# Spreading the attention heads' reciprocal sums over partitions by two DMAs instead of TensorE transposes

## The chip, the cores and the metric

The kernel runs on one core of one Trainium2 chip. The metric is the device time in microseconds from the start of one execution to its end; the median of several executions is compared.

## The reference, cut to what matters

The program is one layer of a decoder trunk: forgetting attention with 16 heads of width 64 over 1,024 tokens of width 1,024, a layer norm, a mixture of 64 experts, and a second layer norm. The change touches the attention alone, and in it the division of a head's weighted values by its sums of exponentials:

```python
logits = einsum('bqhd,bkhd->bhqk', q[:, t0:t1], k[:, :t1]) * scale
logits = logits + c[:, :, t0:t1, None] - c[:, :, None, :t1]
p = softmax(where(causal, logits, -inf), axis=-1)          # per head and query
outs.append(einsum('bhqk,bkhd->bqhd', p, v[:, :t1]))
...
return o @ w_out
```

## The kernel before, in words

All engines are programmed by hand with semaphores; each engine runs its own list of instructions in order and waits where the list says so. Every matrix product is split in a high and a low part, so that one product is three matmuls (`split_matmul`, L91 to L93).

**A head.** `head(p, par)` is one of 16 heads, h = 2p + par. Heads 0 and 1 and the last two are written out, heads 2 to 13 are a loop over pairs. A head has eight steps t, one for each tile of 128 queries. In a step TensorE (PE) makes the scores of that tile (L864 to L867, one or two slots of up to 512 keys; 12 slots in a head), then transposes blocks of exponentials of earlier slots ("turns", L894) and projects a part of the next head's queries and keys (L91 to L93). VectorE (DVE) takes the maxima of the scores (L1681), ScalarE (ACT) the exponentials with their sums (L1290). ACT copies a turned slot out of PSUM as `pt_hi` (L1301), and DVE subtracts for `pt_lo` (L1692).

**The order of the turns** is a table, `TURNS`, and `STEP_TURNS` says which of its entries come in which step. Slots 8 and 9 of the head before are turned in step 0 of the next head, slots 10 and 11 in step 1, slot 0 in step 2, and so on up to slots 6 and 7 in step 7. Turns alternate between the two banks of the PSUM tile `k_ps`; a turn waits until `pt_lo` of the turn before it in its bank is made (`bank_free`).

**The weighted values.** `weigh_v(h, par, half)` (L916) multiplies the values with the turned exponentials of four query tiles into `pv_ps`, half of the PSUM tile `out_ps`. The first half is made in step 7 of head h and the second in step 3 of head h + 1. The result is transposed: 64 partitions hold the head's columns from the values' high part, 64 those of the low part, and the queries lie along the free axis. ACT copies the low part to `heads_sum` (`low_values`, L1309), and DVE adds the high part (`sum_halves`, L1707), which counts `added`. `weigh_v` waits for `added` of the half before, since both use `pv_ps`.

**The reciprocals.** The sums of the exponentials lie the other way, one query per partition: `ssum[par]` is 128 x 2 x 8. `reciprocals` (L1698, L1702) makes `rec[par]`, 128 x 8, half 0 in step 6 of its head and half 1 in step 1 of the next. To multiply `heads_sum` by them, 64 partitions must each hold a row of 512 reciprocals. Before the change PE makes it: the two entries `("rows", -1, 0)` in step 2 and `("rows", -1, 1)` in step 5 of the next head are four transposes each of a column of `rec` read 64 times (L901), into a bank of `k_ps`. `by_rows` (L1714) multiplies `heads_sum` with that bank into `attn`, which is the profile's tile `xs`, and counts `normed`. DVE does `normalise`, that is `sum_halves` and then `by_rows`, for half 0 in step 2 after the turn's `pt_lo` and for half 1 in step 5 before it.

**After the last head** PE turns the last slots, weighs the last half, and goes on with the output projection (`first_tile_out`, `out_projection`). GpSimd (POOL) sits in a wait for `normed` through all of the attention; then it makes constants and fills tables in memory.

**DMAs.** All of the attention's transfers are issued from SP's queue: the next head's weights `wqk`, values `va`, and per half the copies `q_ones` and `k_twice` between partitions.

Of the kernel before, what the change touches and what calls it, by code (L numbers as in the profile page):

```python
# [47 lines left out]
def turned_blocks(n):  # L48
# [47 lines left out]
def build(nc, x, w_in, b_f, w_out, ln1_g, ln1_b, router, router_bias, w_gate, w_up, w_down, ws_gate, ws_up,  # L96
          ws_down, ln2_g, ln2_b, out):
    with ExitStack() as ctx:
# [16 lines left out]
        v_dram = nc.dram_tensor("v_scratch", (T, HEADS, 2 * DH), F32, kind="Internal").ap()  # L115
        c_dram = nc.dram_tensor("c_scratch", (2, HEADS, T), F32, kind="Internal").ap()
# [10 lines left out]
        ones_b = sb("ones_b", [P, P], BF16)  # L127
        before = sb("before", [P, P], BF16)
# [3 lines left out]
        with ExitStack() as early:  # L132
# [3 lines left out]
            with ExitStack() as x1s:  # L136
# [21 lines left out]
                with ExitStack() as b:  # L158
# [5 lines left out]
                    heads_sum = sb("heads_sum", [DH, BANK], c=b)  # L164
# [3 lines left out]
                    rsum = sb("rsum", [P, TT // 2], c=b)  # L168
                    rec = [sb(f"rec{i}", [P, TT], c=b) for i in range(2)]
            with ExitStack() as d:  # L170
# [60 lines left out]
                zeros = sb("zeros", [P, ROW_W], c=d)  # L231
                nblk = [sb(f"nblk{i}", [1, E], c=d) for i in range(2)]
# [53 lines left out]
        for n in ("masks xt_ps xt_hi_ok xt_lo_ok wf_in wf_ok gate_ps g1_in gate_step zexp_ok"  # L286
                  " c_hi_ok c_lo_ok c_stored wv_hi_ok wv_lo_ok v_ps v_hi_ok v_ok"
                  " wqk_hi_ok wqk_lo_ok proj c_in ev_hi ev_lo copied score max_step maxed exped turned_ps turned_hi turned_lo rows_ps rec_step rec_ok"
# [43 lines left out]
        def load_v(sp, h, par):  # L332
            sp.dma_start(va[par][:].bitcast(F32), v_rows[:, :, bass.ds(h, 1), :].rearrange("p t o n -> p t (o n)")).then_inc(va_in[par], 16)

# [37 lines left out]
        def stand(eng):  # L372


            eng.sem_inc(S["stands"], 1)
# [209 lines left out]
        def _(pool):  # L585
# [24 lines left out]


            pool.wait_ge(S["normed"], NORMED)
# [170 lines left out]
        def _(pe):  # L783
# [86 lines left out]
            def bank_free(h, u, there):  # L870

                past = [v for v in range(u - 2, -1, -2) if there(TURNS[v])]
                if past:
                    kind, back, n = TURNS[past[0]]
                    if kind == "turn":
                        pe.wait_ge(S["turned_lo"], NS * h + (NS * back + n + 1))
                    else:
                        pe.wait_ge(S["normed"], 2 * h + (2 * back + n + 1))
# [4 lines left out]
            def turns(h, par, us, first=False, ends=False):  # L883
                for u in us:
                    kind, back, n = TURNS[u]
# [1268 lines left out]
```

## Time and profile before

| | us |
|---|---|
| median of 3 executions | 1645.97 |
| lowest and highest | 1644.61, 1650.76 |
| span of the profiled execution, first to last instruction | 1640.5 |
| attention heads, first scores to last `by_rows` | about 136 to 562 |

The profile gives the span alone of the execution that it shows; a measured time has some microseconds before and after the span too. On the profile's timeline a matmul's duration overlaps the next one's, so that its cost is read from start to start: a 512-column matmul is shown with 0.39 us and the next starts 0.23 us later. A bracket at the end of a line gives the idle time ahead of an instruction and what released it; an instruction can have waited without a bracket, because the modelled end of the one before it covers the wait. `x4` is four instructions merged in one line.

### The profile page before, as it was taken

How to read it: one execution, taken by the hardware profiler on the slowest of the kernel's cores; microseconds unless marked ns; L12 is line 12 of the kernel's file. 1: busy time of each engine (PE TensorE's matmuls, PEld its weight loads, DVE VectorE, ACT ScalarE, POOL GpSimd, SP SyncE). 2: the span in 40 equal slices, each digit the busy share in tenths (PEclk: the TensorE clock that was granted, in tenths of full speed). 3: DMA queues.
4: the chain of work that ended last, by engine and by line, in shares of the span. 5: the costliest groups of instructions: out<-in, count | busy, mean ns of one | idle time of the engine just before them, and what ended most of it. 6: DMA issues, size and time to landing. Idle time of an engine off the chain costs nothing.

```text
span 1640.5 us, 32188 instructions
## 1 busy us (share of the span) xinstructions
PE 1578.0 (96%) x8246; PEld 1310.0 (80%) x8247; DVE 1182.3 (72%) x2036; ACT 1032.5 (63%) x1706; POOL 503.7 (31%) x495
## 2 busy tenths in 40 slices
PE   6999999999999999899999999999999999999986
PEld 6897888888887788778878888888888888888863
DVE  4214777777777788847777787777876787888866
ACT  3214666666666655527677787666776777877854
POOL 0000000000000135432544454543454445454426
PEclk9999999999999999899999999999999999999995
DMA  7223222222123533657999999999999999999987
GB/s 245 91 81 91 72 48 68 58 65 71 45 71 103 170 134 138 227 196 281 337 291 318 305 357 367 326 289 264 334 318 288 274 353 331 342 368 370 367 252 282
DMA packets 161320, 368.63 MB, mean 225 GB/s; under 512 B 53009, under 2 KB 73489, under 8 KB 161265
## 3 DMA queue, kind: packets, MB, share of 16 engines
q1 hardware_dynamic: 136272, 284.21, 49.7%
q0 software_dynamic: 24992, 83.73, 19.7%
q8 instruction: 28, 0.46, 0.1%
q14 instruction: 28, 0.22, 0.0%
HBM read 294.39 MB, written 65.11 MB: 219 GB/s over the span
## 4 chain that ended last, share of the span: by engine, by line
PE 72%; DVE 8%; DMA 8%; issue 5%; ACT 3%; ACTq 2%; POOL 1%; SPq 0%; DVEq 0%; POOLq 0%
PE bank_pair L1025 6%; PE bank_pair L1031 6%; PE bank_pair L1028 6%; DMA sums_scratch<-ys,sidx 5%; PE q_ps L91 4%; PE q_ps L93 4%; PE q_ps L92 4%; PE out_ps L916 4%; PE k_ps L894 4%; PE out_ps L1084 3%; PE out_ps L1085 3%; PE q_ps L1015 3%; PE k_ps L1052 2%; PE k_ps L1053 2%; PE k_ps L1060 2%
## 5 line engine op out<-in xcount | busy, mean ns | idle before, releaser
L1918 DVE TENSOR_TENSOR gu_lo<-raw_gu,gu_hi 128x1024 fp32r<-128x1024 f32 x260 | 306.3, 1220 | 25.5 <-ACT gu_hi L1396 25.5
L1396 ACT CAST gu_hi<-raw_gu 128x1024 fp32r<-128x1024 f32 x260 | 253.2, 1050 | 2.3 <-DMA raw_gu<-in_moe_w_gate_dram 1.5
L1025 PE MATMUL bank_pair<-gu_hi,xb_hi 128*128 128x512 f32 x576 | 233.1, 405 | 5.5 <-DVE gu_lo L1918 4.2
L1028 PE MATMUL bank_pair<-gu_lo,xb_hi 128*128 128x512 f32 x576 | 226.9, 394 | 0.0
L682 POOL DMA_INDIRECT sums_scratch<-ys,sidx x63 | 122.1, 1939 | 148.9 <-DMA sums_scratch<-ys,sidx 116.0
L1918 DVE TENSOR_TENSOR dn_lo<-raw_dn,dn_hi 128x1024 fp32r<-128x1024 f32 x130 | 152.6, 1213 | 2.9 <-ACT dn_hi L1396 2.4
L1031 PE MATMUL bank_pair<-gu_hi,xb_lo 128*128 128x512 f32 x576 | 142.7, 390 | 2.0 <-DVE xb_lo L1922 2.0
L1301 ACT CAST pt_hi<-k_ps 128x512 fp32r<-128x512 f32 (+1 forms) x192 | 85.7, 482 | 75.4 <-PE k_ps L894 74.7
L1025 PEld LDWEIGHTS bank_pair<-gu_hi,xb_hi 128*128 128x128 f32 x576 | 110.1, 191 | 28.8 <-issue 6.4
L613 POOL IOTA e<- 128x64 f32 x1 | 0.2, 185 | 428.8 <-DVE xs L1714 428.8
L1396 ACT CAST dn_hi<-raw_dn 128x1024 fp32r<-128x1024 f32 x130 | 130.0, 1052 | 2.9 <-DMA raw_dn<-in_moe_w_down_dram 2.9
L1031 PEld LDWEIGHTS bank_pair<-gu_hi,xb_lo 128*128 128x128 f32 x576 | 108.0, 188 | 24.8 <-DVE xb_lo L1922 2.4
L1028 PEld LDWEIGHTS bank_pair<-gu_lo,xb_hi 128*128 128x128 f32 x576 | 109.7, 190 | 21.1
L657 POOL DMA_INDIRECT x_rows<-rows_scratch,gidx x64 | 77.4, 1210 | 154.2 <-DVE wcol L1934 122.6
L1692 DVE TENSOR_TENSOR pt_lo<-k_ps,pt_hi 128x512 fp32r<-128x512 f32 (+1 forms) x192 | 100.4, 551 | 27.8 <-ACT pt_hi L1301 27.0
L1052 PE MATMUL k_ps<-dn_hi,ht_hi 128*128 128x512 f32 x288 | 118.4, 411 | 0.0
L1053 PE MATMUL k_ps<-dn_lo,ht_hi 128*128 128x512 f32 x288 | 112.5, 391 | 0.0
L91 PE MATMUL q_ps<-xt_hi,wqk_hi 128*128 128x512 f32 x256 | 109.2, 427 | 0.0
L1290 ACT ACTIVATE probs<-bank_pair,nm 128x512 f32<-128x512 f32 (+3 forms) x128 | 74.7, 586 | 43.2 <-DVE nm L1685 29.7
L1084 PE MATMUL out_ps<-gu_hi,xo 128*128 128x512 f32 x248 | 97.3, 392 | 4.5 <-DVE xo L1938 4.5
L93 PE MATMUL q_ps<-xt_hi,wqk_lo 128*128 128x512 f32 x256 | 100.5, 393 | 0.0
L92 PE MATMUL q_ps<-xt_lo,wqk_hi 128*128 128x512 f32 x256 | 100.3, 392 | 0.0
(306 smaller groups left out, 3973.7 us busy)
## 6 DMA issues: line engine op xcount, KB each, us to landing
raw_gu<-in_moe_w_gate_dram SPq DMA_DIRECT2D x128, 512.0 KB, 6.8
raw_gu<-in_moe_w_up_dram SPq DMA_DIRECT2D x128, 512.0 KB, 8.6
raw_dn<-in_moe_w_down_dram SPq DMA_DIRECT2D x128, 512.0 KB, 8.3
wqk<-in_fox_w_in_dram SPq DMA_DIRECT2D x66, 128.0 KB, 2.5
v_scratch<-v_out SPq DMA_DIRECT2D x32, 256.0 KB, 2.8
va<-v_scratch SPq DMA_DIRECT2D x16, 512.0 KB, 4.7
fin<-sums_scratch SPq DMA_DIRECT2D x16, 512.0 KB, 8.3
xs<-in_x_dram SPq DMA_DIRECT2D x8, 512.0 KB, 7.4
```

The lines of the kernel that those rows point to most:

```text
L91: pe.matmul(out, w_hi, m_hi, start=start, stop=False, skip_group_check=True)
L92: pe.matmul(out, w_hi, m_lo, start=False, stop=False, skip_group_check=True)
L93: return pe.matmul(out, w_lo, m_hi, start=False, stop=stop, skip_group_check=True)
L682: g.indirect_dma_start(out=sums[0], out_offset=bass.IndirectOffsetOnAxis(ap=sidx[par][:, 0:1], axis=0), in_=ys[par][:], in_offset=None, co ...
L1025: i = pe.matmul(o3, xb_hi[s][:, c], g_hi[:, :, c], start=c == 0, stop=False, skip_group_check=True)
L1028: pe.matmul(o3, xb_hi[s][:, c], g_lo[:, :, c], start=False, stop=False, skip_group_check=True)
L1031: i = pe.matmul(o3, xb_lo[s][:, c], g_hi[:, :, c], start=False, stop=c == DC - 1, skip_group_check=True)
L1052: pe.matmul(k_ps[:, r], ht_hi[:, c], d_hi[:, c, r], start=c == 0, stop=False, skip_group_check=True)
L1053: pe.matmul(k_ps[:, r], ht_hi[:, c], d_lo[:, c, r], start=False, stop=False, skip_group_check=True)
L1084: pe.matmul(o3, xo[:, c], g_hi[:, :, c], start=c == 0, stop=False, skip_group_check=True)
L1396: a.copy(hi, raw).then_inc(S[done], 1)
L1918: dve.tensor_tensor(lo, raw, hi, ALU.subtract).then_inc(S[lo_ok], 1)
```

## The change

PE's eight transposes per head are gone, and with them the `rows` entries of `TURNS`; the other turns stay in their steps. POOL, for each head and half, waits for `rec_ok`, stores the 128 x 4 reciprocals to a row of 512 numbers in memory (`rec_scratch`), so that query 128t + p stands at that place, waits for the store, and loads the row into 64 partitions of a new tile `rec_rows`, partitions 0 to 63 for half 0 and 64 to 127 for half 1. Before the store it waits until the load before it has landed and until the multiplication that last used this half of `rec_rows` is done. `by_rows` waits for the load (`rows_in`) and reads `rec_rows` from SBUF instead of the bank. `heads_sum` has 128 partitions now, a half for each half, and ACT's wait in `low_values` is looser by one. Two constants of POOL, `ones_b` and `before`, are made after the attention.

```diff
-TURNS = [("turn", -1, 8), ("turn", -1, 9), ("turn", -1, 10), ("turn", -1, 11), ("turn", 0, 0), ("rows", -1, 0), ("turn", 0, 1),
-         ("turn", 0, 2), ("rows", -1, 1)] + [("turn", 0, n) for n in range(3, 8)]
-STEP_TURNS = [(0, 1), (2, 3), (4, 5), (6,), (7,), (8, 9), (10, 11), (12, 13)]
+TURNS = [("turn", -1, 8), ("turn", -1, 9), ("turn", -1, 10), ("turn", -1, 11), ("turn", 0, 0), ("turn", 0, 1),
+         ("turn", 0, 2)] + [("turn", 0, n) for n in range(3, 8)]
+STEP_TURNS = [(0, 1), (2, 3), (4,), (5,), (6,), (7,), (8, 9), (10, 11)]
...
+        rec_dram = nc.dram_tensor("rec_scratch", (2, BANK), F32, kind="Internal").ap()
...
-                    heads_sum = sb("heads_sum", [DH, BANK], c=b)
+                    heads_sum = sb("heads_sum", [P, BANK], c=b)
+                    rec_rows = sb("rec_rows", [P, BANK], c=b)
...
+            def spread_reciprocals(p, par, first=False):
+
+                h = 2 * p + par
+                for half in range(2):
+                    n = 2 * h + half
+                    pool.wait_ge(S["rec_ok"], n + 1)
+                    if not (first and half == 0):
+                        pool.wait_ge(S["rows_in"], 32 * n)
+                    if not first:
+                        pool.wait_ge(S["normed"], n - 1)
+                    stand(pool)
+                    pool.dma_start(rec_dram[half].rearrange("(t p) -> p t", p=P), rec[par][:, half * 4:half * 4 + 4],
+                                   allow_slow_non_contiguous=True).then_inc(S["rows_in"], 16)
+                    pool.wait_ge(S["rows_in"], 32 * n + 16)
+                    stand(pool)
+                    pool.dma_start(half_rows(rec_rows, half), rec_dram[half:half + 1, :].to_broadcast([DH, BANK])).then_inc(S["rows_in"], 16)
+            spread_reciprocals(0, 0, first=True)
+            spread_reciprocals(0, 1)
+            with pool.Fori(1, PAIRS) as p:
+                for par in range(2):
+                    spread_reciprocals(p, par)
+
+            pool.wait_ge(S["normed"], NORMED)
             g.memset(ones_b[:], 1.0).then_inc(S["c_const"], 1)
...
-                    else:
-                        pe.wait_ge(S["rec_ok"], 2 * h + (2 * back + n + 1))
-                        stand(pe)
-                        for j in range(4):
-                            t = 4 * n + j
-                            i = pe.transpose(bank[0:DH, j * P:(j + 1) * P], rec[of][:, t:t + 1].to_broadcast([P, DH]), ident[:])
-                        i.then_inc(S["rows_ps"], 1)
...
-            turns(HEADS, 0, (2, 3, 5), ends=True)
+            turns(HEADS, 0, (2, 3), ends=True)
             weigh_v(HEADS - 1, 1, 1)
-            turns(HEADS, 0, (8,), ends=True)
             first_tile_out(DC - 1)
...
-                if not (static(h) and 2 * h + half == 0):
-                    act.wait_ge(S["normed"], 2 * h + half)
-                a.copy(heads_sum[:], pv_ps[DH:P, :]).then_inc(S["low_ok"], 1)
+                if not (static(h) and h == 0):
+                    act.wait_ge(S["normed"], 2 * h + (half - 1))
+                a.copy(half_rows(heads_sum, half), pv_ps[DH:P, :]).then_inc(S["low_ok"], 1)
...
-                dve.wait_ge(S["rows_ps"], 2 * h + (half + 1))
-                bank = key_banks[TURNS.index(("rows", -1, half)) % 2]
-                dve.tensor_tensor(attn[par * DH:(par + 1) * DH, bass.ds(p, 1), half * BANK:(half + 1) * BANK], heads_sum[:, None, :],
-                                  bank[0:DH, None, :], ALU.mult).then_inc(S["normed"], 1)
+                dve.wait_ge(S["rows_in"], 64 * h + (32 * half + 32))
+                dve.tensor_tensor(attn[par * DH:(par + 1) * DH, bass.ds(p, 1), half * BANK:(half + 1) * BANK], half_rows(heads_sum, half)[:, None, :],
+                                  half_rows(rec_rows, half)[:, None, :], ALU.mult).then_inc(S["normed"], 1)
```

## Rows read from the trace of the kernel before

**Rows 1.** The page of the profiled execution: its span, and the busy time of each engine.

```profile
span 1640.5 us, 32188 instructions
...
PE 1578.0 (96%) x8246; PEld 1310.0 (80%) x8247; DVE 1182.3 (72%) x2036; ACT 1032.5 (63%) x1706; POOL 503.7 (31%) x495
```

**Rows 2.** Busy time by stretch: PE, PEld, DVE, ACT, POOL, granted clock, DMA share, GB/s.

```profile
180.00:520.00 340.00, 338.26 (x1959) 282.54 (x1958) 258.40 (x545) 221.68 (x583) 0.00 (x0) 1.00 0.25 60
```

**Rows 3.** Timeline of PE, heads 6 and 7: start, us, engine, line, op.

```profile
305.97 0.60 PE L901 MATMUL k_ps<-ident,rec 128*64 128x128 f32 x4
306.40 0.60 PE L894 MATMUL k_ps<-ident,probs 128*128 128x128 f32 x4
...
314.85 0.23 PE L867 MATMUL bank_pair<-mask_qk,identb 128*128 128x128 bf16 x1
315.27 0.98 PE L894 MATMUL k_ps<-ident,probs 128*128 128x128 f32 x7 [0.19 <-DVE pt_lo L1692]
...
318.45 1.04 PE L894 MATMUL k_ps<-ident,probs 128*128 128x128 f32 x8
...
321.93 0.60 PE L901 MATMUL k_ps<-ident,rec 128*64 128x128 f32 x4
322.28 0.48 PE L91 MATMUL q_ps<-xt_hi,wqk_hi 128*128 128x512 f32 x1
...
324.64 0.47 PE L916 MATMUL out_ps<-pt_hi,va 128*128 128x512 f32 x1
```

**Rows 4.** Timeline of DVE in the same stretch.

```profile
305.71 1.02 DVE L1681 TENSOR_REDUCE nm<-bank_pair 128x1 f32<-128x512 f32 x2 [0.55 <-PE bank_pair L865]
...
307.82 0.68 DVE L1714 TENSOR_TENSOR xs<-heads_sum,k_ps 64x512 f32 x1 [0.27 <-DVE heads_sum L1707]
...
312.39 0.69 DVE L1627 TENSOR_TENSOR wqk_lo<-wqk,wqk_hi 128x512 fp32r<-128x512 f32 x1 [1.12 <-ACT wqk_hi L1251]
313.00 0.17 DVE L1698 RECIPROCAL rec<-ssum 128x4 f32<-128x4 f32 x1
...
314.46 1.01 DVE L1692 TENSOR_TENSOR pt_lo<-k_ps,pt_hi 128x512 fp32r<-128x512 f32 x2
...
321.11 0.18 DVE L1702 RECIPROCAL rec<-rsum 128x4 f32<-128x4 f32 x1
321.73 0.69 DVE L1672 SCALAR_TENSOR_TENSOR q_both<-q_ps,q_both 64x512 fp32r<-64x512 f32 x1 [0.44 <-ACT k_twice L1282]
...
323.82 0.67 DVE L1707 TENSOR_TENSOR heads_sum<-out_ps,heads_sum 64x512 f32<-64x512 f32 x1
324.64 0.68 DVE L1714 TENSOR_TENSOR xs<-heads_sum,k_ps 64x512 f32 x1
```

**Rows 5.** Timeline of ACT in the same stretch.

```profile
311.75 0.61 ACT L1251 CAST wqk_hi<-wqk 128x512 fp32r<-128x512 f32 x1
```

**Rows 6.** Timeline of PE where the last head begins.

```profile
520.57 0.23 PE L867 MATMUL bank_pair<-mask_qk,identb 128*128 128x128 bf16 x1
520.63 0.94 PE L894 MATMUL k_ps<-ident,probs 128*128 128x128 f32 x7
```

**Rows 7.** Timeline of all engines after the last head.

```profile
556.34 0.60 PE L901 MATMUL k_ps<-ident,rec 128*64 128x128 f32 x4 [1.65 <-DVE pt_lo L1692]
...
557.04 0.68 DVE L1714 TENSOR_TENSOR xs<-heads_sum,k_ps 64x512 f32<-64x512 f32 x1 [0.85 <-PE k_ps L901]
```

**Rows 8.** DVE groups by line and form, 180 to 520 us: count, busy us, mean ns.

```profile
L1627 DVE TENSOR_TENSOR wqk_lo<-wqk,wqk_hi 128x512 fp32r<-128x512 f32 x26 | 18.0, 692 | 15.0 <-ACT wqk_hi L1251 13.9
```

**Rows 9.** DMA issues of the whole run: count, KB each, median us to landing.

```profile
sums_scratch<-ys POOLq DMA_DIRECT2D x8, 512.0 KB, 4.1
```

**Rows 10.** DMA issues from 180 to 520 us.

```profile
q_ones<-q_both SPq DMA_DIRECT2D x26, 128.0 KB, 3.1
```

**Rows 11.** The tile tab_scratch: ns min/median/max of the issues, us to landing.

```profile
L635 POOL DMA_INDIRECT tab_scratch<-tok,dest_i x64: 965/969/1967, 595.8 to 719.3; - x64
...
DMA to landing us min/median/max: 2.1/2.4/7.1
```

More of the change, by code:

```diff
@@ L231, in build @@
                 zeros = sb("zeros", [P, ROW_W], c=d)
+                ones_b = sb("ones_b", [P, P], BF16, c=d)
+                before = sb("before", [P, P], BF16, c=d)
                 nblk = [sb(f"nblk{i}", [1, E], c=d) for i in range(2)]
@@ L287, in build @@
                   " c_hi_ok c_lo_ok c_stored wv_hi_ok wv_lo_ok v_ps v_hi_ok v_ok"
[L288 removed]
+                  " wqk_hi_ok wqk_lo_ok proj c_in ev_hi ev_lo copied score max_step maxed exped turned_ps turned_hi turned_lo rows_in rec_step rec_ok"
                   " pv low_ok added normed"
@@ L333, in load_v, with half_rows @@
             sp.dma_start(va[par][:].bitcast(F32), v_rows[:, :, bass.ds(h, 1), :].rearrange("p t o n -> p t (o n)")).then_inc(va_in[par], 16)
+        def half_rows(tile, half):
+            return tile[half * DH:(half + 1) * DH, :]
         def copy_halves(sp, h, par, half):
@@ L873, in bank_free @@
                 if past:
-                    kind, back, n = TURNS[past[0]]
-                    if kind == "turn":
-                        pe.wait_ge(S["turned_lo"], NS * h + (NS * back + n + 1))
-                    else:
-                        pe.wait_ge(S["normed"], 2 * h + (2 * back + n + 1))
+                    _, back, n = TURNS[past[0]]
+                    pe.wait_ge(S["turned_lo"], NS * h + (NS * back + n + 1))
                 elif not (static(h) and h == 0):
@@ L884, in turns @@
                 for u in us:
-                    kind, back, n = TURNS[u]
+                    _, back, n = TURNS[u]
                     if first and back:
                         continue
-                    of = par if back == 0 else 1 - par
                     bank = key_banks[u % 2]
                     bank_free(h, u, lambda x: not (first and x[1]) and not (ends and not x[1]))
-                    if kind == "turn":
-                        pe.wait_ge(S["exped"], NS * h + (NS * back + n + 1))
-                        for j in range(SLOTS[n][2] // P):
-                            i = pe.transpose(bank[:, j * P:(j + 1) * P], probs[n % PROBS][:, j * P:(j + 1) * P], ident[:])
-                        i.then_inc(S["turned_ps"], 1)
-                    else:
-                        pe.wait_ge(S["rec_ok"], 2 * h + (2 * back + n + 1))
-                        stand(pe)
-                        for j in range(4):
-                            t = 4 * n + j
-                            i = pe.transpose(bank[0:DH, j * P:(j + 1) * P], rec[of][:, t:t + 1].to_broadcast([P, DH]), ident[:])
-                        i.then_inc(S["rows_ps"], 1)
+                    pe.wait_ge(S["exped"], NS * h + (NS * back + n + 1))
+                    for j in range(SLOTS[n][2] // P):
+                        i = pe.transpose(bank[:, j * P:(j + 1) * P], probs[n % PROBS][:, j * P:(j + 1) * P], ident[:])
+                    i.then_inc(S["turned_ps"], 1)
             def weigh_v(h, par, half):
@@ L1327, in head @@
                     for u in STEP_TURNS[t]:
-                        if TURNS[u][0] == "turn" and not (first and TURNS[u][1]):
+                        if not (first and TURNS[u][1]):
                             turned_high(h, u)
@@ L1739, in head @@
                     for u in STEP_TURNS[t]:
-                        if TURNS[u][0] == "turn" and not (first and TURNS[u][1]):
+                        if not (first and TURNS[u][1]):
                             turned_low(h, u)
```

10 lines of the change are left out of this document (3 added, 7 removed).

## The prediction

> **What bounds the kernel now.** I read the page first. TensorE is busy for 96% of a span of 1640.5 us [rows 1], so any work taken from it looks like time. The windows come next, because a share over the whole span says nothing of one stage: through the heads PE is busy for 338.26 of 340.00 us at a granted clock of 1.00, DVE for 258.40, ACT for 221.68, and POOL does nothing [rows 2]. That again says PE. But a matmul's end is modelled and can hide a wait, so the third view is the timeline, read from start to start on PE, then on DVE and ACT for the same microseconds. The reader should look there at two places in each head at which PE waits for DVE though it is shown busy.
>
> *Place 1, step 0.* The last score matmul of head 7's step 0 starts at 314.85 and the turn of slot 8 at 315.27 [rows 3]. Where nothing is waited for these two lie 0.06 us apart [rows 6]. So PE stood still for 0.36 us, for `pt_lo` of slot 6, the first of the two that start at 314.46 [rows 4]. That wait has a history. DVE begins the maxima of step 5 at 305.71, having waited 0.55 us for PE's scores; goes through `heads_sum`, `by_rows` at 307.82 and the maxima of step 6; ACT makes the exponentials of step 6 from those and then `wqk_hi` at 311.75 [rows 5]; DVE waits 1.12 us for it, makes `wqk_lo` at 312.39, the maxima of step 7, and `pt_lo` at 314.46 [rows 4]. From 305.71 to 315.27 that chain takes 9.56 us; PE's own work beside it, from 305.97 to 314.91, takes 8.94.
>
> *Place 2, step 3.* `weigh_v` of the second half starts at 324.64 [rows 3], 0.15 us after `heads_sum` of half 0 ended on DVE at 323.82 + 0.67 = 324.49 [rows 4]: it may not overwrite `pv_ps` before. This chain begins with PE's turn of slots 10 and 11 at 318.45 [rows 3], goes through ACT's copies, exponentials and `k_twice`, for which DVE waited 0.44 us at 321.73, and through `k_rest`, the maxima of step 2 and `pt_lo` of slot 0 to `heads_sum` [rows 4].
>
> The timeline repeats this: the step-0 wait stands in heads 1 to 14 (0.2 to 0.4 us), the step-3 wait in all of heads 1 to 15. Only the start of head 15 has no wait: 520.57 to 520.63 [rows 6]. A head takes (520.63 - 315.27) / 8 = 25.67 us [rows 3, 6].
>
> **The change part by part.**
>
> *Transposes removed.* The four of half 1 in step 5 cost 306.40 - 305.97 = 0.43 us, the four of half 0 in step 2 cost 322.28 - 321.93 = 0.35 us [rows 3]. With 16 of each that is 16 x 0.78 = 12.5 us of PE time. Where they lie decides what it is worth.
>
> - Step 5, heads 1 to 13. They stand at 305.97, behind the scores that start DVE's chain at 305.71, and ahead of place 1. They shorten the 8.94 us and not the 9.56. PE comes 0.43 us earlier and waits 0.79 instead of 0.36. Worth 0.
> - Step 2, heads 1 to 15. They stand at 321.93, after the turn that starts the second chain and ahead of place 2. `heads_sum` does not need them, so `weigh_v` starts when it did. Worth 0; at the most the 0.1 us by which PE's wait there can be smaller than it looks.
> - Step 5 of head 14. Nothing is waited for at 520.63 [rows 6], since head 14 splits no further weights in step 6. Worth 0.43 us, which the following turns hand on.
> - Step 5 of head 15. There the output weights are split and PE waits for DVE's `wo_lo`. Worth 0.
> - After head 15. Four transposes at 556.34 stand straight ahead of `weigh_v`, and DVE's `by_rows` waited 0.85 us for them [rows 7]. Four more follow `weigh_v`. PE gains 2 x 0.35 = 0.7 at most. But the first tile's layer norm follows the last `by_rows`, which moves only by the 0.35 of `weigh_v`, and PE needs that tile next. I take 0.5, between the bounds 0.35 and 0.7.
>
> *by_rows.* It now reads both operands from SBUF. The nearest row of that form is `wqk_lo<-wqk,wqk_hi`, 692 ns [rows 8], against 680 ns for `by_rows` [rows 4]. In step 5 it lies in the chain of place 1: 13 x 0.012 = 0.2 us slower at most.
>
> By the Trainium skill (VectorE: DVE Perf Modes, The TRN2 errata — SBUF-src ops pay a fixed extra latency per instruction) VectorE pays 58 cycles fixed from SBUF and 120 from PSUM at 0.96 GHz, so `by_rows` would get 65 ns shorter and the kernel, as an estimate from that page, 13 x 0.065 = 0.8 us faster instead of 0.2 slower. The two rows of this case differ by 12 ns the other way, and they decide the sum.
>
> *Store and load.* No row shows such a pair. The store is 512 pieces of 4 bytes. The nearest row is POOL's scatter of 128 pieces of 4 bytes: landing 2.4 us after the issue starts, 2.1 at least and 7.1 at most, its issue 0.97 [rows 11]. If only the issue grows with the pieces, it is 4 x 0.97 - 0.97 = 2.9 us longer. I take 2.4 + 1.7 = 4.1. The load is 128 KB in 64 rows. SP's transfers of that form land in 3.1 us [rows 10], POOL's of 512 KB in 4.1 [rows 9]. I take 3.5. With two semaphore hops a pair takes X = 7.8 us. Lower bound 2.1 + 3.1 = 5.2; upper bound 7.1 + 4.1 = 11.2, or with the longer issue on top 14.1.
>
> What covers it: half 0's `rec` is ready at 313.17 and its `by_rows` starts at 324.64, 11.5 us later. Half 1's is ready at 321.29 and used in the next head at 307.82 + 25.67 = 333.5, 12.2 us later [rows 3, 4, 6]. But POOL does them one after the other: both pairs, from 313.17, must be through by 333.5, so 2X must be under 20.3 us and X under 10.2. With 7.8 nothing is late: cost 0, and 4.7 us to spare. Queued behind POOL's waits are only its constants, which nobody needs until after the attention. SP's queue keeps its order.
>
> *Other waits.* ACT's looser wait in `low_values` and the freer bank of `k_ps` bind nowhere in the loop. The two constants made later, on POOL, run while `dest_i` is far off. Worth 0.
>
> *Sum.* Against the profiled execution: 1640.5 - 0.43 - 0.5 + 0.1 = 1639.7. The median of the runs, 1645.97, lies 5.5 us above that span; the same distance gives 1645.1.
>
> **The rivals.**
>
> *A: PE really is the bound.* If the waits at places 1 and 2 shrink with PE's work, because DVE and ACT run on as PE feeds them earlier, all 12.5 us come: 1645.97 - 12.5 = 1633.5. For it: 96% and 338.26 of 340.00. If only the step-2 part came, 15 x 0.35 = 5.3 us: 1640. Against it: the chain of place 1 begins before the transposes, and DVE's own maxima keep ACT from starting sooner.
>
> *B: the rows come late (the other side).* X over 10.2. Then `by_rows` of half 1 waits on DVE, in front of `pt_lo` of slot 3 and the maxima of step 6, straight in the chain of place 1. ACT waits for these maxima and PE for `pt_lo`. Each head loses 2X - 20.3. It decides from X = 10.5, where 14 x 0.6 = 8.2 us are lost. At X = 11.2 it is 2.1 a head, 14 x 2.1 = 29: 1675. For it: a landing of 7.1 us for 4-byte pieces [rows 11] and four times as many pieces here. Against it: that was the maximum and the median is 2.4, and DMA is a quarter busy in this stretch [rows 2].
>
> The Trainium skill (SBUF — State Buffer, SBUF: two separate sides) has a rule that points this way: POOL's DMAs are described by software that cannot write descriptors while DVE runs a two-port copy. In the heads DVE runs no copy or cast, and no row has a POOL DMA here, so it is open. A wait for one DVE instruction of 0.69 us [rows 4] at each of the two DMAs would make X 9.2, still under 10.2.
>
> *C: the small packets disturb SP's copies.* `q_ones` and `k_twice` of half 1 are issued about when half 1's store is. They land in 3.1 us [rows 10] and step 4 needs them about 6 us after the issue. Were they 3 us late and 0.6 more, a head would lose 0.6: 1654.
>
> **How the numbers follow.** A half per cent, 8.2 us, is about what a measurement of this kernel tells from no change. Forecast 0.72, within 1643.5 and 1646.5: both places of PE's wait are read off three engines, and the cover of the DMAs is some 30% longer than they need. A 0.12, of which 0.10 full. B 0.12, C 0.04. A's small form at 1640 is inside the half per cent, so faster is 0.10, same 0.74, slower 0.16. The range reaches down to 1633 to take in A, and up to 1654, B's and C's beginning; it leaves out the rest of B, about 0.1, and some of A.
>
> **What would show it.** Right: no L901; PE's busy time about 12 us lower through the heads and the period of a head still 25.6 to 25.8; gaps before the step-0 turn near 0.8 us and before `weigh_v` near 0.5; `by_rows` never released by a DMA; store to landing of load 7 to 9 us. Wrong: a period near 24.9 (A); DVE's `xs` waiting for a DMA, a longer period (B); PE's step-4 scores released by `k_twice` (C). What would make me wrong above all is the price of 512 four-byte pieces, which no row has, or a chain on DVE and ACT that moves up with PE after all.

## The result, and the profile after

The changed kernel takes 1800.57 us (median of 4, 1794.85 to 1802.99) against 1646.53 for the kernel before beside it: 1.0932 times as long, 95% interval 1.0906 to 1.0958. It is slower by 154 us where 1645.1 was forecast.

Page of the changed kernel: span and busy times, the granted clock in 40 slices, the chain that ended last, the two groups of part 5 in which the loss stands (busy us and mean ns, then the idle time ahead and its releaser), and the values' DMA of part 6.

```profile
span 1796.9 us, 32138 instructions
PE 1604.8 (89%) x8118; PEld 1322.5 (74%) x8119; DVE 1187.9 (66%) x2036; ACT 1032.2 (57%) x1706; POOL 558.0 (31%) x559
PEclk9999898988888988998999999999999999999995
PE 38%; DMA 29%; issue 8%; DVE 8%; ACT 4%; ACTq 1%; POOL 1%; POOLq 1%; DVEq 1%; another core or an unknown queue 1%
DMA rec_scratch<-rec 15%; DMA rec_rows<-rec_scratch 8%; PE bank_pair L1036 5%; PE bank_pair L1039 5%; PE bank_pair L1042 5%; DMA sums_scratch<-ys,sidx 4%; PE out_ps L1095 3%; PE out_ps L1096 3%; PE q_ps L1026 3%; PE k_ps L1063 2%; PE k_ps L1064 2%; PE k_ps L1071 2%; DVE gu_lo L1928 2%; PE out_ps L1113 2%; PE out_ps L1114 1%
L913 PE MATMUL k_ps<-ident,probs 128*128 128x128 f32 x576 | 93.2, 286 | 106.0 <-DVE pt_lo L1703 105.9
L1724 DVE TENSOR_TENSOR xs<-heads_sum,rec_rows 64x512 f32 (+1 forms) x32 | 22.0, 686 | 137.4 <-DMA rec_rows<-rec_scratch 136.4
va<-v_scratch SPq DMA_DIRECT2D x16, 512.0 KB, 11.8
```

The new store and load hold 23% of the chain that ended last. DVE waited 136.4 us for the rows, and PE then 105.9 us for the `pt_lo` behind them. The window of [rows 2] now reads:

```profile
180.00:520.00 340.00, 260.76 (x1354) 211.37 (x1353) 193.17 (x398) 161.96 (x425) 25.69 (x40) 0.87 0.27 54
```

PE is busy for 260.76 us in place of 338.26, and has done 1354 instructions in place of 1959. One head on POOL's timeline (start, us, then in brackets the idle time ahead and what ended it), and the lines of DVE and PE at its end:

```profile
399.99 0.79 POOL L621 DMA_DIRECT2D rec_scratch<-rec  x1 [10.99 <-DVE rec L1709]
408.62 0.53 POOL L625 DMA_DIRECT2D rec_rows<-rec_scratch  x1 [7.85 <-DMA rec_scratch<-rec]
413.01 0.79 POOL L621 DMA_DIRECT2D rec_scratch<-rec  x1 [3.85 <-DMA rec_rows<-rec_scratch]
423.02 0.53 POOL L625 DMA_DIRECT2D rec_rows<-rec_scratch  x1 [9.23 <-DMA rec_scratch<-rec]
434.87 0.79 POOL L621 DMA_DIRECT2D rec_scratch<-rec  x1 [11.32 <-DVE rec L1709]
```
```profile
399.07 0.17 DVE L1709 RECIPROCAL rec<-ssum 128x4 f32<-128x4 f32 x1
...
412.48 0.68 DVE L1724 TENSOR_TENSOR xs<-heads_sum,rec_rows 64x512 f32 x1 [1.15 <-DMA rec_rows<-rec_scratch]
...
428.76 0.69 DVE L1724 TENSOR_TENSOR xs<-heads_sum,rec_rows 64x512 f32 x1 [7.64 <-DMA rec_rows<-rec_scratch]
...
433.95 0.17 DVE L1709 RECIPROCAL rec<-ssum 128x4 f32<-128x4 f32 x1
```
```profile
430.23 0.47 PE L913 MATMUL k_ps<-ident,probs 128*128 128x128 f32 x1 [7.32 <-DVE pt_lo L1703]
```

The loss can be read off these lines. Half 0's reciprocals are ready at 399.07 + 0.17 = 399.24, and half 1's `by_rows` starts at 428.76. In between lie 0.75 us up to the first store's issue, then store (8.63), load (4.39), store (10.01) and load (5.74), one after the other: 29.5 us. The kernel before left 20.3 us for them. This head is a usual one: from store to load it is 8.1 to 11.2 us over all 32 stores, 9.8 at the median. From that `by_rows` to the next reciprocals' end takes 434.12 - 428.76 = 5.36 us, as before (313.17 - 307.82 = 5.35, [rows 4]). So a head takes 29.5 + 5.4 = 34.9 us in place of 25.7 [rows 3, 6], 9.2 more, and 16 x 9.2 = 147. The last `by_rows` ends at 712.2, against 562.0 before: 150 of the 154 us are in the heads.

The clock fell with the waits. Windows of the same kernel:

```profile
402.50:408.50 6.00, 6.00 (x37) 5.13 (x35) 3.94 (x9) 4.40 (x12) 0.00 (x0) 1.00 0.00 0
```
```profile
420.00:425.00 5.00, 2.91 (x17) 2.17 (x15) 1.05 (x3) 2.31 (x6) 0.53 (x1) 1.00 0.40 56
425.00:430.00 5.00, 0.00 (x0) 0.00 (x0) 1.21 (x2) 0.00 (x0) 0.00 (x0) 0.56 0.42 106
430.00:435.00 5.00, 4.77 (x13) 3.49 (x14) 3.67 (x9) 2.11 (x6) 0.13 (x1) 0.50 0.00 0
```

PE waited 7.32 us up to its matmul at 430.23, and within that wait the granted clock went from 1.00 to 0.50, that is from 2.4 to 1.2 GHz. It costs little here: DVE's part of the head took the same 5.36 us. The first of these lines shows something odder. From 402.5 to 408.5 the store has not yet released POOL, and yet the DMA engines' busy share is 0.00 and 0 GB/s move. From 399.9 to 408.6 the profile counts these packets for POOL's queue (packets, MB, share):

```profile
q0 software_dynamic: 32, 0.00, 0.7%
```

So all the packets that it shows of the store lie ahead of 402.5, and some 6 us pass after them in which it shows nothing. What takes the time is not carrying bytes.

### The profile page after: what moved, and what is told of

It is laid out like the page before. It is cut to its first block, busy times and chain, and to the rows that moved or that the text cites. A ratio compares the mean times of both kernels' runs of the same rounds, so it can differ in the third digit from the quotient of the medians.

```text
span 1796.9 us, 32138 instructions
## 1 busy us (share of the span) xinstructions
PE 1604.8 (89%) x8118; PEld 1322.5 (74%) x8119; DVE 1187.9 (66%) x2036; ACT 1032.2 (57%) x1706; POOL 558.0 (31%) x559
## 4 chain that ended last, share of the span: by engine, by line
PE 38%; DMA 29%; issue 8%; DVE 8%; ACT 4%; ACTq 1%; POOL 1%; POOLq 1%; DVEq 1%; another core or an unknown queue 1%
DMA rec_scratch<-rec 15%; DMA rec_rows<-rec_scratch 8%; PE bank_pair L1036 5%; PE bank_pair L1039 5%; PE bank_pair L1042 5%; DMA sums_scratch<-ys,sidx 4%; PE out_ps L1095 3%; PE out_ps L1096 3%; PE q_ps L1026 3%; PE k_ps L1063 2%; PE k_ps L1064 2%; PE k_ps L1071 2%; DVE gu_lo L1928 2%; PE out_ps L1113 2%; PE out_ps L1114 1%
## 5 line engine op out<-in xcount | busy, mean ns | idle before, releaser
L913 PE MATMUL k_ps<-ident,probs 128*128 128x128 f32 x576 | 93.2, 286 | 106.0 <-DVE pt_lo L1703 105.9
L913 PEld LDWEIGHTS k_ps<-ident,probs 128*128 128x128 f32 x576 | 66.1, 148 | 110.2 <-DVE pt_lo L1703 109.9
L681 POOL DMA_INDIRECT x_rows<-rows_scratch,gidx x64 | 81.8, 1278 | 146.3 <-DVE wcol L1944 115.4
L91 PE MATMUL q_ps<-xt_hi,wqk_hi 128*128 128x512 f32 x256 | 116.0, 453 | 0.0
L1724 DVE TENSOR_TENSOR xs<-heads_sum,rec_rows 64x512 f32 (+1 forms) x32 | 22.0, 686 | 137.4 <-DMA rec_rows<-rec_scratch 136.4
L93 PE MATMUL q_ps<-xt_hi,wqk_lo 128*128 128x512 f32 x256 | 107.1, 418 | 0.0
L92 PE MATMUL q_ps<-xt_lo,wqk_hi 128*128 128x512 f32 x256 | 106.9, 418 | 0.0
```

The lines of the kernel that those rows point to most:

```text
L91: pe.matmul(out, w_hi, m_hi, start=start, stop=False, skip_group_check=True)
L92: pe.matmul(out, w_hi, m_lo, start=False, stop=False, skip_group_check=True)
L93: return pe.matmul(out, w_lo, m_hi, start=False, stop=stop, skip_group_check=True)
L913: i = pe.transpose(bank[:, j * P:(j + 1) * P], probs[n % PROBS][:, j * P:(j + 1) * P], ident[:])
```

## The experiments

The loop issues 32 stores and 32 loads in all, one pair for each half of the 16 heads; where an expectation says 64 pairs or 64 stores, it is 32. "The heads end" is the end of the last `by_rows`, 562.0 us in the kernel before; it compares also where the output of the heads differs, and with it the experts' counts and the time behind the heads. It holds for one execution, and the first reciprocals of these executions lie between 154.5 and 158.6 us (158.3 in the kernel before), so that a difference of some 4 us says little. "A head" is the distance of half 0's reciprocals from heads 2 to 14, divided by 12.

**Is it the size of the pieces?** In this run each partition's four reciprocals go to memory as one piece of 16 bytes, and `by_rows` undoes the order by reading `rec_rows` with a step of four numbers.

```diff
-pool.dma_start(rec_dram[half].rearrange("(t p) -> p t", p=P), rec[par][:, half * 4:half * 4 + 4],
-               allow_slow_non_contiguous=True).then_inc(S["rows_in"], 16)
+pool.dma_start(rec_dram[half].rearrange("(p t) -> p t", p=P), rec[par][:, half * 4:half * 4 + 4]).then_inc(S["rows_in"], 16)
...
-dve.tensor_tensor(attn[par * DH:(par + 1) * DH, bass.ds(p, 1), half * BANK:(half + 1) * BANK], half_rows(heads_sum, half)[:, None, :],
-                  half_rows(rec_rows, half)[:, None, :], ALU.mult).then_inc(S["normed"], 1)
+dve.tensor_tensor(attn[par * DH:(par + 1) * DH, bass.ds(p, 1), half * BANK:(half + 1) * BANK].rearrange("q o (t p) -> q (o t) p", p=P),
+                  half_rows(heads_sum, half).rearrange("q (t p) -> q t p", p=P),
+                  half_rows(rec_rows, half).rearrange("q (p t) -> q t p", p=P), ALU.mult).then_inc(S["normed"], 1)
```

> The store writes each partition's four reciprocals as one piece of 16 bytes (128 pieces instead of 512 of 4 bytes), and by_rows reads rec_rows with a step of four, so that the result is the same. If the number of 4-byte pieces is the price: the store lands 2.5 to 3.5 us after its issue instead of 8 to 10, a pair takes about 7, nothing is late, and the time is 1645 +- 2, since by the prediction's steps the removed transposes are worth about 1 us. If PE's work was the bound after all: 1633. If any store and load on POOL's queue is slow whatever its pieces: about 1800 as with the change.

Measured: 1656.73 us, 1.0052 times the kernel before (1.0038 to 1.0066). Nearly all of the 154 us are gone. POOL's timeline of this run:

```profile
319.05 0.57 POOL L621 DMA_DIRECT2D rec_scratch<-rec  x1 [14.56 <-DVE rec L1708]
322.31 0.53 POOL L624 DMA_DIRECT2D rec_rows<-rec_scratch  x1 [2.69 <-DMA rec_scratch<-rec]
```

From store to load it is 3.26 us in place of 8.6 to 10. What is left has another cause: the heads end at 575.6, 13 us late, and DVE's groups of 180 to 520 us show it:

```profile
L1723 DVE TENSOR_TENSOR xs<-heads_sum,rec_rows 64x512 f32 (+1 forms) x26 | 27.9, 1072 | 7.0 <-DVE heads_sum L1717 5.9 <-DMA rec_scratch<-rec 1.1
```

Read with a step, `by_rows` takes 1072 ns in place of 686, and 32 x 0.386 = 12.4 us is about the delay.

**What are the removed transposes worth?** No DMA at all; `rec_rows` is filled once with a constant, so that the heads are not normalised.

```diff
-            spread_reciprocals(0, 0, first=True)
-            ...
+            pool.wait_ge(S["rec_ok"], 1)
+            g.memset(rec_rows[:], 0.01).then_inc(S["rows_in"], 1)
...
-                dve.wait_ge(S["rows_in"], 64 * h + (32 * half + 32))
+                dve.wait_ge(S["rows_in"], 1)
```

> The change without its two DMAs: rec_rows is filled once with a constant, so the values are not normalised by their sums. This is what the removed transposes are worth by themselves. By the prediction's steps (both places shadowed by the DVE and ACT chain): 1645 +- 2, a head still 25.6 to 25.8 us, the gap before the step-0 turn near 0.8 us. If PE's work sets the pace: 1633.5, a head 24.9.

Measured: 1662.38 us for the kernel, ratio 1.0086 (1.0069 to 1.0103). The 14 us lie behind the heads, whose output is another one here; the heads end at 562.8. Window:

```profile
180.00:520.00 340.00, 330.86 (x1842) 268.25 (x1841) 257.64 (x540) 220.77 (x581) 0.00 (x0) 1.00 0.25 60
```

PE is busy for 7.4 us less here than in [rows 2] and stands still for as much longer; the heads end no sooner, and from their first reciprocals they take 406.7 us against 403.7 before. Taken away alone, the transposes were worth nothing.

**What do the DMAs do when `by_rows` does not wait for them?** The kernel before, transposes included, with POOL's stores and loads as in the change, and `by_rows` reading PE's rows. One wait stays, in the last line: DVE's `reciprocals` may overwrite `rec` only when the load of two heads before has landed (in the runs without a load, the store). "Unwaited" below means this.

```diff
+            spread_reciprocals(0, 0, first=True)
+            spread_reciprocals(0, 1)
+            with pool.Fori(1, PAIRS) as p:
+                for par in range(2):
+                    spread_reciprocals(p, par)
...
+                if not (static(h) and h < 2):
+                    dve.wait_ge(S["rows_in"], 64 * h + (32 * half + 32 - 128))
```

> The kernel before, transposes and all, and beside them POOL's stores and loads of the change into a tile that nobody reads. Nobody waits for them, except that rec is not overwritten two heads later before its store has gone. If the loss of the change is that by_rows waits for the rows: 1646 to 1650. If it is that the small pieces hold up SP's copies (q_ones, k_twice, which landed up to 11.6 us after issue with the change and are needed some 6 us after it): up to 5 us a head more, 1690 to 1720, with PE's or DVE's waits put down to k_twice or q_ones.

Measured: 1728.83 us, ratio 1.0483 (1.0465 to 1.0500), 80 us slower. The heads end at 617.6, 56 us late; POOL itself, behind with its pairs, comes out of them only at 667.0, and the stage behind the heads needs it. The waits of this run from 200 to 520 us (total, times, longest):

```profile
POOL rec_rows L622 <- DMA rec_scratch<-rec: 192.9, 19, 11.2
...
PE bank_pair L886 <- DMA k_twice<-k_twice: 23.5, 8, 5.6
```

Not all of the 80 us is a disturbance of other transfers. The pairs take longer than a head, POOL falls behind, and the one wait that stayed binds in the last heads (136 to 720 us):

```profile
DVE ssum L1724 <- DMA rec_rows<-rec_scratch: 20.0, 4, 11.1
DVE rec L1722 <- DMA rec_rows<-rec_scratch: 1.6, 1, 1.6
```

That is 21.6 of the 56 us in the heads, and the other 24 of the 80 come behind them, where POOL is late. Some 34 us are left for what the transfers do to others.

**Is it the number of pieces?** The changed kernel with 128 pieces of 4 bytes per store instead of 512, loaded four times over, so that the rows of all but one tile of 128 queries are another tile's.

```diff
-pool.dma_start(rec_dram[half].rearrange("(t p) -> p t", p=P), rec[par][:, half * 4:half * 4 + 4],
+pool.dma_start(rec_dram[half, 0:P].rearrange("(p t) -> p t", p=P), rec[par][:, half * 4:half * 4 + 1],
```

> The change with a store of only one of the four columns of reciprocals, 128 pieces of 4 bytes, repeated four times by the load (256 pieces of 512 bytes): three quarters of the queries get another tile's reciprocal. If the price goes with the number of pieces: the store lands after about 3.5 us (2 us fixed and a quarter of the 7 us above it), nothing is late, 1645. If it goes with 4-byte writes as such: 8 us and about 1800.

Measured: 1844.09 us, ratio 1.1188 (1.1166 to 1.1209); the heads end at 726.4. A quarter of the pieces, and POOL's timeline shows a store that is hardly cheaper:

```profile
407.70 0.54 POOL L621 DMA_DIRECT2D rec_scratch<-rec  x1 [11.04 <-DVE rec L1709]
415.06 0.63 POOL L625 DMA_DIRECT2D rec_rows<-rec_scratch  x1 [6.82 <-DMA rec_scratch<-rec]
421.57 0.54 POOL L621 DMA_DIRECT2D rec_scratch<-rec  x1 [5.88 <-DMA rec_rows<-rec_scratch]
430.56 0.63 POOL L625 DMA_DIRECT2D rec_rows<-rec_scratch  x1 [8.44 <-DMA rec_scratch<-rec]
```

7.4 and 9.0 us from store to load, and 8.6 at the median of all 32 against 9.8. A price per piece falls with this run. That the heads end even later than with the change (712.2) goes with the load: it is written in four parts here and takes 6.5 us (415.06 to 421.57) in place of 4.4. What the dear stores have in common is that their 4-byte pieces lie packed, one beside the other, so that is what the next three runs vary, unwaited.

**Unwaited, 16 bytes.** The run of 1728.83 with the 16-byte store of the first one.

> The kernel before, with TensorE's turned reciprocals as they were, and the 64 pairs of store and load issued on Pool's queue with nobody waiting for their data: the same as the run that cost 1728.8 us with 4-byte pieces, but each store now writes 128 pieces of 16 bytes. Theory (what is dear is a run of 4-byte writes packed densely in memory, which holds up the other transfers of the queues): the stores land in under 3 us, the copies of q and k on SP's queue keep their 3.1 us, and the kernel is at 1646 to 1651. Rival (any store and load every 12.8 us disturbs SP's copies, 64-fold broadcast included): at least 1680. A small disturbance that the changed kernel's own waits had covered would stand between, near 1655.

Measured: 1642.40 us, ratio 0.9968 (0.9953 to 0.9984); store landing 2.5 us after its issue at the median. Nothing is disturbed by 32 pairs as such, the broadcast loads included. That the ratio lies under 1 is not explained: the heads end at 561.4 as before.

**Unwaited, 4 bytes, each in 64 bytes of its own, no load.**

```diff
-rec_dram = nc.dram_tensor("rec_scratch", (2, BANK), F32, kind="Internal").ap()
+rec_dram = nc.dram_tensor("rec_scratch", (2, BANK * 16), F32, kind="Internal").ap()
...
-pool.dma_start(rec_dram[half].rearrange("(t p) -> p t", p=P), rec[par][:, half * 4:half * 4 + 4],
+pool.dma_start(rec_dram[half].rearrange("(t p s) -> p t s", p=P, s=16)[:, :, 0], rec[par][:, half * 4:half * 4 + 4],
```

> The kernel before plus 64 unread stores on Pool's queue and no load: 512 pieces of 4 bytes as in the change, but each piece in 64 bytes of its own (the scratch tensor is 16 times as large). Theory A (pieces that share a stretch of memory are written one after another): the store lands in 3 to 4 us and the kernel is at 1646 to 1652. Theory B (4-byte writes are dear as such, wherever they lie): the store keeps its 8 to 10 us and the kernel is at 1700 to 1730. The run with 128 pieces, which kept 8.2 us, speaks against a price per piece, so A is thought likelier, at 60 to 40.

Measured: 1644.42 us, ratio 0.9974 (0.9954 to 0.9993). The tile's view:

```profile
L618 POOL DMA_DIRECT2D rec_scratch<-rec x32: 752/752/989, 159.5 to 551.2; - x32
...
DMA to landing us min/median/max: 2.2/3.1/3.6
```

The same 512 pieces, the same bytes, the same issue time, and a landing of 3.1 us.

**Unwaited, 4 bytes packed, no load.** As the last one, with the change's own store.

> The kernel before plus the same 64 unread stores of 512 dense 4-byte pieces, and no load. Theory (the store alone is what holds up SP's transfers): most of the 80 us of the run with both transfers stay, 1700 to 1730. Rival (the 64-fold broadcast load of 128 KB, 64 packets more per pair, is the disturbing part): under 1665.

Measured: 1677.41 us, ratio 1.0176 (1.0144 to 1.0208); the heads end at 591.6. Less than expected: the packed store alone costs 29 us. That is near the 34 that were left of the 80 for disturbed transfers; the load behind a cheap store cost nothing (1642.40). What the load adds behind a dear one was not taken apart further. The 29 us do not come evenly: six of the fifteen distances from head to head are 4.6 to 6.4 us longer than in the kernel before, the other nine as they were. The DMA issues from 200 to 650 us (count, KB each, median us to landing), and one of the places at which PE pays:

```profile
q_ones<-q_both SPq DMA_DIRECT2D x26, 128.0 KB, 4.9
k_twice<-k_twice SPq DMA_DIRECT2D x26, 128.0 KB, 5.5
```
```profile
416.60 0.50 PE L883 MATMUL bank_pair<-k_twice,q_both 128*128 128x512 f32 x1 [4.04 <-DMA k_twice<-k_twice]
```

All of PE's waits for `k_twice` in this run, from 200 to 520 us:

```profile
PE bank_pair L883 <- DMA k_twice<-k_twice: 13.5, 4, 4.0
```

SP's copies land in 3.2 us each in the same stretch of the kernel before. Here they take 4.9 and 5.5, though they are on another queue, and the slowest `k_twice` 13.2 in place of 4.7. The Trainium skill (DMA: Bandwidth & Descriptors, Back-pressure in remote DMA) says that stalled writes stall the other queues of the same DMA engine too. It says so of transfers between cores; this run's landings, 5.5 in place of 3.2, agree for local ones.

**The place in memory, in the changed kernel itself.** All of the change kept, its waits, load and DVE's multiplication; each 4-byte piece in 64 bytes of its own, by the same edit; ahead of the heads two DMAs fill the larger tensor once. The load reads the first 512 numbers of that larger tensor, so the heads are not normalised by their own sums.

> The changed kernel with its 512 pieces of 4 bytes per store, its waits, its load of 128 KB and its multiplication on DVE all kept; only each piece lies in 64 bytes of its own. The load reads the first 512 words of that tensor, which hold few of the reciprocals, so the heads are not normalised, and the counts of the experts behind them differ: the end of the heads is what compares (562.0 us in the kernel before, 711.5 plus 0.69 in the changed one). Theory (the whole loss is the dense 4-byte store): store and load together take 7 us, nobody waits, the heads end at 562 to 566. Rival (512 packets and a broadcast load with waits between them cost of themselves, in the changed order of the instructions): the heads end beyond 580.

Measured: 1646.87 us, ratio 1.0016 (0.9999 to 1.0034); the heads end at 565.1. POOL's timeline:

```profile
401.10 0.79 POOL L621 DMA_DIRECT2D rec_scratch<-rec  x1 [4.37 <-DVE rec L1716]
404.74 0.53 POOL L625 DMA_DIRECT2D rec_rows<-rec_scratch  x1 [2.85 <-DMA rec_scratch<-rec]
```

Of the 150 us in the heads 147 hang on where 512 small pieces lie. The load, too, is faster behind such a store: it lands in 2.8 us at the median. In this run the change behaves as forecast, in time too, though the counts of the experts behind the heads are not the same.

**The order of instructions, in the kernel before.** If the two places bind, moving their chains forward should help. The first two edits are ScalarE's, the last is DVE's.

```diff
-                        take(h, par, 1)
                         low_values(h - 1, 0)
+                        take(h, par, 1)
...
-                    elif t == 6 and left > 2:
+                    elif t == 5 and left > 2:
                         weights_hi(h + 2, 0)
...
                     if t == 2 and not first:
-                        normalise(h - 1, *before_it, 0)
+                        by_rows(h - 1, *before_it, 0)
                     if t == 1 and not first:
                         reciprocals(h - 1, 1 - par, 1)
+                        sum_halves(h - 1, 0)
```

> The kernel before with its transposes and three instructions of the chain DVE/ScalarE moved: the high weights of head h+2 from step 6 to step 5 of ScalarE, the low copy of head h-1 ahead of the score copy in step 1, and the sum of its two halves on DVE from step 2 to step 1. If the two places where TensorE waits in each head (step 0's turn for the low part, step 3's values for the sum) are what bounds the heads, about 0.2 to 0.4 us per head come off: 1635 to 1643. If TensorE's own work is the bound there, 1646 to 1650 as before.

Measured: 1650.39 us, ratio 1.0015 (1.0003 to 1.0028): no gain. PE's timeline shows why:

```profile
316.03 0.23 PE L867 MATMUL bank_pair<-mask_qk,identb 128*128 128x128 bf16 x1
316.10 0.94 PE L894 MATMUL k_ps<-ident,probs 128*128 128x128 f32 x7
...
325.01 0.23 PE L867 MATMUL bank_pair<-mask_qk,identb 128*128 128x128 bf16 x1
325.59 0.44 PE L894 MATMUL k_ps<-ident,probs 128*128 128x128 f32 x2 [0.35 <-DVE pt_lo L1692]
325.81 0.47 PE L916 MATMUL out_ps<-pt_hi,va 128*128 128x512 f32 x1
```

In step 0 the wait is gone: 0.07 us between the first two lines, where it was 0.42 [rows 3]. In step 3 `weigh_v` comes 0.22 us after its turn's start, where it was 0.37. But that turn itself now waits 0.5 us for a `pt_lo`, which is as much as was won at both places.

**A version that lets the transposes count.** The changed kernel with the 16-byte store, and `by_rows` on POOL, which is free there. POOL does it behind its load of the same half, and DVE's `reciprocals` wait until the multiplication two heads before is through (last line), since it no longer stands in DVE's own order.

```diff
+            def by_rows(h, p, par, half):
+                pool.wait_ge(S["added"], 2 * h + (half + 1))
+                pool.wait_ge(S["rows_in"], 64 * h + (32 * half + 32))
+                g.tensor_tensor(attn[par * DH:(par + 1) * DH, bass.ds(p, 1), half * BANK:(half + 1) * BANK].rearrange("q o (t p) -> q (o t) p", p=P),
+                                half_rows(heads_sum, half).rearrange("q (t p) -> q t p", p=P),
+                                half_rows(rec_rows, half).rearrange("q (p t) -> q t p", p=P), ALU.mult).then_inc(S["normed"], 1)
...
+                if not (static(h) and h < 2):
+                    dve.wait_ge(S["normed"], 2 * h + (half - 3))
```

> The changed kernel with two changes: the store writes 128 pieces of 16 bytes, and the multiplication by the rows (32 in all, one per half of a head) is done by Pool, which reads the rows with a step of four words, in place of DVE. TensorE's transposes stay removed. Theory (with cheap stores and no transposes the chain of DVE and ScalarE sets the pace of the heads, as the lengthened multiplication showed: 32 times 0.385 us by its step, and the heads ended 12.9 us later): taking 0.686 us twice a head off DVE lets TensorE's removed 12.5 us come through in part; the heads end at 552 to 558 us in place of 562.0 and the kernel is at 1636 to 1642. Rival 1 (the two places are held by other waits, the values' results for one): no gain, heads end at 562 to 565, 1645 to 1650. Rival 2 (Pool at work beside DVE slows DVE's own instructions): over 1652.

Measured: 1644.19 us, ratio 0.9988 (0.9975 to 1.0002). The heads end at 563.6, as in rival 1, 12 us before the same kernel with DVE's long `by_rows` and no sooner than the kernel before.

**Both together.** The same with the order of instructions moved as above (`by_rows` has left DVE, so `sum_halves` alone moves there).

> The kernel of the 16-byte store with Pool's multiplication, and the order of instructions moved as in the run of the reordered kernel before (that run: 1650.4 us, no gain): high weights of head h+2 in step 5 of ScalarE, the low copy of head h-1 ahead of the score copy in step 1, the sum of the halves on DVE in step 1. Theory: with TensorE's 12.5 us of transposes gone the waits at the two places are all that is left, so the moved instructions now help: 2 to 6 us below the same kernel without the reorder. Rival: they only move the wait to another step, as in the kernel before: within 2 us of it.

Measured: 1624.27 us, ratio 0.9863 (0.9842 to 0.9885). This beats both kernels, the one before by 22 us and the changed one by 176. The heads end at 547.6. Tile `rec` on DVE from 200 to 520 us, half 0's line, in the kernel before, in the run without the moved instructions and in the one with them:

```profile
L1698 DVE RECIPROCAL rec<-ssum x13: 167/171/174, 210.0 to 516.9; 128x4 f32<-128x4 f32 x13
```
```profile
L1718 DVE RECIPROCAL rec<-ssum x13: 167/171/172, 208.9 to 516.0; 128x4 f32<-128x4 f32 x13
```
```profile
L1718 DVE RECIPROCAL rec<-ssum x13: 164/170/172, 206.5 to 498.9; 128x4 f32<-128x4 f32 x13
```

A head takes (516.9 - 210.0) / 12 = 25.58 us in the kernel before, (516.0 - 208.9) / 12 = 25.59 with POOL's `by_rows` alone, and (498.9 - 206.5) / 12 = 24.37 with both edits: 1.21 less than before. PE's time for a head's transposes was 0.78, and its waits at the two places, as the prediction reads them, 0.36 and 0.15: 1.29 in all. So the transposes and the waits seem to come through together, and only here. PE is full again; its window of this run:

```profile
180.00:495.00 315.00, 313.68 (x1806) 263.51 (x1805) 241.40 (x503) 215.41 (x567) 67.95 (x78) 1.00 0.33 76
```

**Which of the two edits carries it?** The 16-byte store, DVE's own strided `by_rows`, and the moved instructions.

> The changed kernel with the 16-byte store and DVE's own multiplication (1.07 us, as in the run of the 16-byte store, 1656.7 us, heads ended about 575.7), and the three instructions moved as in the run with Pool's multiplication that came to 1624.3. It tells which of the two edits of that run carries its gain. If the moved instructions alone let TensorE's removed transposes come through: 1638 to 1644 (the 20 us of that run's reorder off 1656.7 would give 1637). If DVE must be relieved of the multiplication too: the strided 1.07 us twice a head keep DVE's chain the pace and the kernel stays at 1650 to 1657.

Measured: 1655.15 us, ratio 1.0043 (1.0028 to 1.0059); the heads end at 569.6. Neither does alone. By the heads' end, from 575.6 with the 16-byte store only: the order gives 6, POOL's `by_rows` 12, both together 28. By the head it is 26.42 us with the store only, 25.97 with the order, 25.59 with POOL's `by_rows`, 24.37 with both. That fits two places in a head, each of which holds it while the other is mended; which edit frees which place was not read off the traces.

## Why the prediction was wrong, point by point

*What bounds the heads: right.* The chains of DVE and ACT at the two places hold PE, not its own work. PE is shown busy for 99% of the window, and the run without DMAs bears out that its work does not set the pace. So does the long `by_rows`: 12.4 us more on DVE and the heads ended 13 us later. One size was off. Without DMAs PE's wait in step 0 of head 7 was to grow from 0.36 to 0.79 us and grew to 0.42 only, while the one ahead of `weigh_v` grew from 0.15 to 0.58.

*Transposes removed, worth 0.9 us: right to within 4.* The heads end at 562.8 against 562.0 without any DMA, and counted from their own beginning they take 3 us more. Rival A falls: it gave 12.5 us, and none came. Its gain comes once DVE and ACT are relieved at both places, which took both edits together (1624.27).

*by_rows 12 ns slower: close.* 686 ns against 680. It decides against the shorter access to SBUF that the prediction takes from the Trainium skill, as the two rows did there.

*Store and load, X = 7.8 us: this is the step that failed.* Measured: 29.5 us for two pairs, X = 14.8. The load was sized at 3.5 and took 4.4 and 5.7. The store was sized at 4.1 and took 8.6 and 10.0, over every bound that was worked out for it alone; only "with the longer issue on top", X = 14.1, came near. Two things were wrong in it. The scatter of [rows 11] was taken as the nearest row, because its pieces are of 4 bytes; but it is a different pattern, each of whose pieces goes to a place that an index gives, and no row of it shows what packed pieces cost. And the price was scaled by the number of pieces, in the issue. The issue grew to 0.79 us only, and with 128 pieces the store was nearly as dear as with 512. What counts is that 4-byte pieces are packed: in 64 bytes of their own the same 512 let the load go 3.64 us after the store's issue in the changed kernel. The load's excess hangs on the same: behind such a store it lands in 2.8 us, under the 3.5.

The Trainium skill (DMA: Bandwidth & Descriptors, Specifications) says that below 512 bytes a DMA engine reads, modifies and writes. It spoke against this change, and the prediction did not weigh it. The runs bear out only a part: pieces of 16 bytes (2.5 us) and of 4 bytes apart (3.1) are both far under 512 bytes and cheap.

*The cover, 20.3 us for two pairs, and rival B's 2X - 20.3 a head: right, with the wrong X.* 29.5 - 20.3 = 9.2 us a head, and the heads end 150 us late for 147 by this term. Rival B was priced only up to X = 11.2, and its chance of 0.12 rested on the median of a row that was not like the store. (Its formula gives 0.7 us a head at X = 10.5, not the 0.6 that stands there.)

*Rival C, the copies disturbed: real, and sized too small.* 9 us were given to it. Unwaited, the packed stores alone cost 29 us, and with their loads some 34 of the 80 are of this kind. In the changed kernel it hides behind B: `k_twice` lands in 6.7 us there (median, 200 to 650 us), but PE waits for it once, for 0.3 us, since it is late already.

What stays open is the mechanism. The store's time passes with the DMA engines shown idle; that the writes wait for one another in memory is a guess that no run shows. Whether pieces must share 64 bytes for that, or only a small stretch (2 KB against 32 KB in the runs apart), no run tells, since both were changed at once. Nor does a run tell apart the 16-byte pieces' size and their number within such a stretch.

## What to carry to other kernels

If small numbers must be spread over partitions through memory, let the store write a contiguous piece per partition, or pieces that lie apart, which were the cheap forms here; undo the order where it is read, on an engine that has time. Where no row of a profile shows a transfer's pattern of addresses, its price is unknown whatever its bytes and pieces are, and if a chain waits for two of them in a row, the range must say so. And work taken from an engine that is shown 99% busy can gain nothing until each chain that it waits for is relieved as well: here, counted from the kernel with the 16-byte store, two edits gave 28 us together, and 6 and 12 singly.

## What the runs showed of the hardware that was not expected

- A store of 128 x 4 numbers of 4 bytes packed in 2 KB took 8.1 to 11.2 us to the next instruction of its queue (median 9.8), with 128 pieces 7.4 to 10.3 (8.6); with each piece in 64 bytes of its own it landed in 3.1 us, as 128 pieces of 16 bytes in 2.5 (medians, unwaited).
- Of the 8.6 us of one such store, the DMA engines show nothing in the last six.
- With such stores under way, transfers of another queue land later: SP's 128 KB copies in 4.9 and 5.5 us in place of 3.2, the 512 KB of values in 8.4 in place of 4.7 (medians, 200 to 650 us).
- DVE's 64 x 512 multiplication takes 686 ns with both operands contiguous and 1072 ns where one is read and all are walked as 4 x 128 with a step of four numbers; POOL needs 1547 ns for the same, and DVE's own instructions beside it kept their lengths (`pt_lo` 551 ns in both kernels).
